# Feed-forward products by seven block products instead of eight: one inference step of a hybrid encoder on one core

## The reference

```python
for layer in range(2):
    h = rms_norm(x, norm_mix[layer])
    mix = ab_mixer(h, ...) if layer == 0 else chunk_mlp_mixer(h, ...)
    x = x + mix
    h = rms_norm(x, norm_ffn[layer])
    f, sc = conv_ffn(h, s_conv[layer], w_in_ffn[layer], ffn_conv_w[layer], ffn_conv_b[layer], w_out_ffn[layer])
    x = x + f
y = rms_norm(x, norm_final)

def conv_ffn(h, conv_hist, w_in, conv_w, conv_b, w_out):      # D_MODEL 1024, D_FF 2816
    proj = h @ w_in                                          # 1024 x 5632
    a, gate = proj[..., :D_FF], proj[..., D_FF:]
    full = concatenate([conv_hist, a])                       # along time
    conv = conv_b + sum(full[:, j:j + T] * conv_w[j] for j in range(3))
    y = (gelu(conv) * gate) @ w_out                          # 2816 x 1024
    return y, full[:, -2:]
```

## Time and profile before

| | |
|---|---|
| timed runs of the kernel before | 2838.18 us median (2835.65, 2838.18, 2838.43) |
| the profiled execution: span | 2835.0 us, 44317 instructions |
| its own time outside the span | not recorded apart; the median lies 3.2 us above the span |
| TensorE busy | 2809.9 us |
| VectorE, ScalarE, GpSimd busy | 1477.7, 707.6, 733.5 us |
| moved | 130.70 MB, 46 GB/s on average |

### The profile page before, as it was taken

The page is one execution under the profiler, slowest core; times in us unless marked ns, Lnnn a source line. Parts: engine busy times, 40 slices in busy tenths (PEclk is TensorE's granted clock), DMA queues, the critical chain, the costliest instruction groups (busy, mean ns, idle before and its releaser), DMA issues.

```text
span 2835.0 us, 44317 instructions
## 1 busy us (share of the span) xinstructions
PE 2809.9 (99%) x16164; PEld 2735.6 (96%) x16164; DVE 1477.7 (52%) x2678; ACT 707.6 (25%) x1191; POOL 733.5 (26%) x540
## 2 busy tenths in 40 slices
PE   9999999999999999999999999999999999999999
PEld 9999999999999999999888999999999999999997
DVE  3658975554444444457323755556544444444454
ACT  4424463211111111114222221214211111111114
POOL 3233325322222222223001230013422222222220
PEclk9999999999999999999999999999999999999999
DMA  4111001111111111111211111111111111111112
GB/s 146 41 43 40 24 27 48 41 42 41 44 41 41 42 43 41 41 45 45 60 51 58 34 42 41 44 41 34 52 42 41 44 41 41 44 41 41 44 48 85
DMA packets 195026, 130.70 MB, mean 46 GB/s; under 512 B 8876, under 2 KB 186741, under 8 KB 194677
## 3 DMA queue, kind: packets, MB, share of 16 engines
q1 hardware_dynamic: 194900, 129.43, 15.2%
q10 hardware_dynamic: 32, 0.01, 0.0%
HBM read 120.60 MB, written 8.81 MB: 46 GB/s over the span
## 4 chain that ended last, share of the span: by engine, by line
PE 94%; DVE 4%; issue 1%; ACT 1%; DMA 0%; POOL 0%; DVEq 0%; SPq 0%; ACTq 0%; POOLq 0%
PE bank L723 49%; PE bank L748 21%; PE bank L1246 7%; PE bank L772 3%; PE bank L884 3%; PE bank L1170 2%; PE bank L1353 2%; PE bank L919 1%; PE bank L822 1%; PE bank L1306 1%; DVE qsc L1548 1%; DVE work L2050 0%; PE bank L1138 0%; DVE sct L1569 0%; PE bank L905 0%
## 5 line engine op out<-in xcount | busy, mean ns | idle before, releaser
L2836 POOL TENSOR_TENSOR raw<-raw,vec 128x512 f32<-128x512 f32 x248 | 279.5, 1138 | 1297.2 <-DMA raw<-in_w_in_ffn 844.3
L723 PE MATMUL bank<-xh,wh 128*128 128x384 f32 x2664 | 607.2, 335 | 0.7 <-issue 0.7
L723 PE MATMUL bank<-xl,wh 128*128 128x384 f32 x2664 | 604.5, 334 | 0.0
L723 PE MATMUL bank<-xh,wl 128*128 128x384 f32 x2664 | 604.4, 334 | 0.0
L2181 ACT ACTIVATE wh<-raw 128x512 fp32r<-128x512 f32 x374 | 235.3, 629 | 1396.3 <-PE bank L723 781.1
L1398 DVE TENSOR_TENSOR wl<-raw,wh 128x512 fp32r<-128x512 f32 x374 | 283.7, 759 | 424.9 <-ACT wh L2181 424.9
L723 PEld LDWEIGHTS bank<-xh,wh 128*128 128x128 f32 x2664 | 473.6, 188 | 2.8 <-issue 1.5
L723 PEld LDWEIGHTS bank<-xl,wh 128*128 128x128 f32 x2664 | 474.6, 188 | 0.0
L723 PEld LDWEIGHTS bank<-xh,wl 128*128 128x128 f32 x2664 | 474.4, 188 | 0.0
L1424 DVE TENSOR_TENSOR xs<-bank,xs 128x384 f32<-128x384 f32 (+1 forms) x648 | 320.9, 550 | 280.3 <-PE bank L748 246.8
L748 PE MATMUL bank<-yh,wh 128*128 128x384 f32 x1152 | 265.0, 338 | 0.0
(11 more groups left out here) (340 smaller groups left out, 3369.6 us busy)
## 6 DMA issues: line engine op xcount, KB each, us to landing
raw<-in_w_in_ffn SPq DMA_DIRECT2D x176, 256.0 KB, 2.9
raw<-in_w_out_ffn SPq DMA_DIRECT2D x88, 256.0 KB, 2.7
raw<-in_w_uv_c SPq DMA_DIRECT2D x64, 256.0 KB, 2.8
raw<-in_w_in_ab SPq DMA_DIRECT2D x40, 256.0 KB, 2.9
raw<-in_w_out_c SPq DMA_DIRECT2D x32, 256.0 KB, 2.7
xtok<-in_x_prompt SPq DMA_DIRECT2D x8, 512.0 KB, 7.7
raw<-in_w_out_ab SPq DMA_DIRECT2D x16, 256.0 KB, 2.7
out_y_prompt<-otok SPq DMA_DIRECT2D x8, 512.0 KB, 2.6
```

The source lines that it names most:

```text
L723: mm = pe.matmul(ps[(sg + tb) % BANKS][:, 0:TB], w[:, place, k * P:(k + 1) * P], r[:, kk, tbs(tb)], start=kk == 0 and c == 0, stop=kk == K ...
L2836: pool.tensor_tensor(r, r, g, ALU.mult).then_inc(w_scaled, 1)
```

## The change

Both feed-forward stages are rewritten. The tokens are cut into two halves of 576 (`HT`, `T1S` and `T2S`), each matmul has 288 columns (`CH`), and PSUM is used as four pairs of banks (`psp`), 288 columns on either side of the middle of a pair.

**Up part.** 22 blocks of 256 columns (an a block, a gate block, in turn), each a product of 2 x 2 blocks: k in two halves, columns in two halves, tokens in two halves. Seven products (`UP_ORDER`) replace eight. Their x operands are x or sums of x blocks, made once per layer by VectorE (`normed`, `combos`), with x normalized and scaled by the gain first, in place, and split (`combo_high`, `combo_low`) into `cw` and `cx`, which take the room of the hidden work and of `xh`, `xl`. Four sums of the weights per block are VectorE's (`first_sums`, `up_sum`); ScalarE and VectorE combine the products as they take them out of PSUM (`up_evict`). GpSimd no longer scales weights.

**Through memory.** `xs` is stored to a scratch tensor in HBM before it is overwritten, and comes back later; all of y is stored as it is made and read back, block by block, into `yb11`, `yb22`, `yb12`, `yb21`.

**Down part.** It now follows the whole up part: seven products (`DOWN_ORDER`) of 11 steps each. A step has a weight piece or the sum of two (`w_sum`, VectorE) and a y block or the sum of two (`y_sum`, GpSimd), and 24 matmuls into four PSUM pairs; after 11 steps VectorE adds the pairs to one or two quarters of `xs` each (`down_evict`). Rings of three and four pieces hold the split operands.

**Edges.** The first product needs the norm. Stage v's split of x starts after the down part; the last layer's down part is like the first's, and the final norm follows it, with x turned by 72 transposes. The feed-forward loops are written out, with no hardware loop.

```diff
@@ TensorE
-                    for u in range(4):
-                        unit(xh, xl, n1 + 12 * i + 2 * u, g1 + 36 * i + 3 * u, n1 + 2 * u, g1 + 3 * u)
-                    down(n1 + 12 * i + 8, g1 + 36 * i + 12, n1 + 8, g1 + 12, 2 * i + (done0 + 2))
-                loop(pe, STEPS - 2, step)
...
+                def product(n, j):
+                    q, pos = UP_ORDER[j], 7 * n + j
...
+                    pe.wait_ge(f_high, done + pos + 1)
+                    pe.wait_ge(f_low, done + pos + 1)
...
+                    for k in range(4):
...
+                        for e, (w, part) in enumerate(((fh, 0), (fh, 1), (fl, 0))):
+                            for c in range(2):
+                                mm = pe.matmul(bank[:, M0 + c * CH:M0 + (c + 1) * CH], w[:, pos % RING, k * P:(k + 1) * P],
+                                               x[:, m, part, c * CH:(c + 1) * CH], start=first and k == 0 and e == 0,
...
+                for j in range(7):
+                    r0 = STEPS * j
+                    for first, last in ((0, 2), *((k, k + 1) for k in range(2, STEPS - 2)), (STEPS - 2, STEPS)):
+                        for f in range(4):
+                            for kk in range(first, last):
+                                down_step(r0 + kk, f)
@@ VectorE
+                inv_rms(1 + 2 * l)
+                dve.wait_ge(x_moved, 160 * l + 16 * KD)
+                for d in range(4):
+                    normed(d, T1S)
+                for k in range(4):
+                    combo_low(0, k)
+                for k in range(4):
+                    normed(k, T2S)
+                    normed(4 + k, T2S)
+                    normed(4 + k, T1S)
+                    combos(k)
+                    combo_low(1, k)
...
+                for pos in range(1, UPS):
+                    if 2 <= pos < 7:
+                        for k in range(4):
+                            combo_low(pos, k)
+                    if pos + 2 < UPS:
+                        up_sum(pos + 2)
...
+                    up_evict(pos - 1)
+                    convs(pos)
+                    if pos + 2 < UPS:
+                        up_low(pos + 2)
...
+                for r in range(2, DOWNS):
+                    j, kk = divmod(r + 1, STEPS)
+                    if kk == 2 and j:
+                        w_low(r)
+                        y_low(r)
+                        down_evict(j - 1)
+                        w_sum(r + 1)
+                    else:
+                        if r + 1 < DOWNS:
+                            w_sum(r + 1)
+                        w_low(r)
+                        y_low(r)
@@ GpSimd
+                for i in range(STEPS):
+                    y_prod(i)
+                for r in range(STEPS, DOWNS):
+                    y_sum(r)
+                    j, kk = divmod(r, STEPS)
...
+                    if l == 0 and j == 6 and 4 <= kk <= 9:
+                        for m in (2 * kk - 8, 2 * kk - 7):
+                            add_square(24 * 2 + m, m % 2, m % NTB, sq_b)
@@ SyncE
+                for d in range(KD):
+                    sp.wait_ge(acc_free, g0 + NTB * (d + 1))
+                    sp.dma_start(xscr[l][d], xs[:, d, :]).then_inc(x_moved, 16)
...
+                        if d >= 8:
+                            sp.wait_ge(f_low, done + UPS + step_of(d - 8) + 1)
...
+                y_tiles(yb22[:, 9:11, :], 20, 22, T2S, y_back[2])
+                for d in range(0, KD, 4):
+                    sp.dma_start(xs[:, d:d + 4, :], xscr[l][d:d + 4].rearrange("d p t -> p d t")).then_inc(x_moved, 16)
@@ the end
+            def finish(t):
...
+                for d in range(KD):
+                    mm = pe.transpose(psp[t % 4][:, d * P:(d + 1) * P], xs[:, d, t * P:(t + 1) * P], ident[:, :])
...
+                dve.scalar_tensor_tensor(otok[:, t % 2, :], psp[t % 4][:, :], fin_sums[:, t, 2:3], fin_gain[:, :],
+                                         ALU.mult, ALU.mult).then_inc(y_out, 1)
```

More of the change, by code:

```diff
@@ new lines, in ring, with y_block, up_sums, sums_of @@
+        def ring(r):
+            e = (3, 1, 2, 0)[r % 4]
+            return (fh3[:, :], fl3[:, :], flf3[:, :]) if e == 3 else (fh[:, e, :], fl[:, e, :], flf[:, e, :])
+        def y_block(b, kk):
+            if b == 21 and kk == STEPS - 1:
+                return yb21_last[:, :]
+            return {11: yb11, 12: yb12, 21: yb21, 22: yb22}[b][:, kk, :]
+        def up_sums(l, n, which):
+            return (4 * PAIRS + len(SUMMED_W) * STEPS) * l + 4 * n + which + 1
+        def sums_of(r, which):
+            j, kk = divmod(r, STEPS)
+            return STEPS * sum(q in which for q in DOWN_ORDER[:j]) + kk + 1
@@ L1393, in _ @@
+            for t in range(NT):
+                finish(t)
         @block.vector
@@ L1815, in abo @@
                         low(n0 + 4 * i + 2 * u + 1, n0 + 2 * u + 1)
-                    if not first or u:
+                    if (not first or u) and not (last and u):
                         low(n0 + 4 * i + 2 * u + 2, n0 + 2 * u + 2)
@@ new lines, in ring_free, with w_sum @@
+                def ring_free(r):
+                    if r:
+                        dve.wait_ge(f_done, done + UPS + r - 3)
+                def w_sum(r):
+                    q = DOWN_ORDER[r // STEPS]
+                    if q not in SUMMED_W:
+                        return
+                    (ra, va), (rb, vb) = (down_raw(l, down_load(r, b)) for b in range(2))
+                    dve.wait_ge(raw_loaded[ra], va)
+                    dve.wait_ge(raw_loaded[rb], vb)
+                    ring_free(r)
+                    dve.tensor_tensor(ring(r)[2], fraw[:, ra, :], fraw[:, rb, :],
+                                      ALU.subtract if q in (6, 7) else ALU.add).then_inc(f_summed, 1)
@@ L2554, in _, with abo @@
             n0, g0, t0 = PLAN.at["abo"]
-            def abo(i):
-                first = isinstance(i, int)
+            def abo(i, first=False, last=False):
                 for u in range(2):
-                    if not first or u:
+                    if (not first or u) and not (last and u):
                         for p, tk in ((2, 1), (3, 4)):
@@ L2669, in _ @@
             rms(2)
-            tail_rows(0)
             def mixing_matrix(m):
```

1272 lines of the change are left out of this document (724 added, 548 removed).

## The result

Changed kernel: **2822.02 us** median (2818.73 to 2823.6, 4 runs); before, on the same chip, 2837.48 us (2835.65 to 2838.43, 4 runs). Ratio 0.9945, 95% interval 0.9931 to 0.9959. The forecast was 2821. The profiled execution has a span of 2818.8 us, against 2835.0.

What follows compares the result with a forecast made beforehand. TensorE, busy 99% of the span, was taken as the bound. Layer 0 at 817.5 against 830.7, stage v giving back 10, and layer 1 at 831 against 845.4 made a span of 2817; 3.2 more gave 2821 us, range 2783 to 2860.

Steps and rivals of the forecast that it cites:

- 5544 matmuls a layer: Both feed-forwards: 288-column matmuls at 0.1342 us each take 744.0 us a layer, against 827.8 before.
- opening: Start of each feed-forward: products wait for the norm and VectorE's split of x; 40 us a layer.
- joint of up and down: Passage from up to down part: steps 0 and 1 end at 18.6 us instead of 9.6; 9 us a layer.
- transfers in the first stage: First down stage: 13.7 MB at 361 GB/s take 38 us against 35.4; 5 us a layer charged.
- both-sum stages: Down stages of products 1, 6 and 7: steps need 3.12 us, under 3.22; 2 us each, 6 us a layer.
- x copied away: Layer 0's opening: the copy of x to memory ends 2.5 us after the reciprocals; 2.5 us.
- squares in layer 0's last stage: Layer 0's last down stage: twelve additions of squares hold VectorE; 8 us.
- stage v: Start of stage v: x split only after the down part, norm at 32 us instead of 21.6; 10 us.
- end: After the last down step: final norm paced by two output buffers; 24 us, against 5.2 before.
- the rival on transfers: First down stage: queue moves 270 GB/s instead of 361, stage takes 51 us; total 2841, no change; chance 0.14.
- Port: Down stages: rival has VectorE and GpSimd alternate whole durations, both-sum step 3.54 us; total 2857, slower; chance 0.17.
- the rival of fewer stalls: Feed-forwards: pitch 0.1332 us, and 14 us a layer for jitter, boundaries and transfers hidden; total 2783; chance 0.18.

Runs made afterwards that it cites:

- e6: Changed kernel with layer 1's up matmuls from block 4 on cut to 256, 192 or 128 columns in turn; 0.112 us a matmul at 192 and 128.
- e3: Changed kernel with VectorE making weight piece 3's low part after the next four low parts of x in each opening; 2820.74 us, ratio 0.9937.
- e1: Changed kernel with x loaded back from memory in two halves, beside up block 3 and early in the second down stage; 2810.56 us, ratio 0.9901.
- e9: e1 with SyncE's transfers around the first down stage reordered, all of y11 ahead of the weights of steps 2 and 3; 2797.19 us, ratio 0.9860.
- e5: Changed kernel with GpSimd adding the y blocks a second time in layer 1's fifth down stage; that stage 45.9 us against 36.44, span 2833.4.
- e7: Changed kernel without GpSimd's twelve additions of squares in layer 0's last down stage; that stage 36.52 us against 45.05.
- e8: Changed kernel with six buffers instead of two for the last twelve squares at stage v's start; 2821.91 us, ratio 0.9945.
- e11: e10 plus e3's opening order, four output tiles instead of two, and a new start of stage v with six square buffers; 2772.98 us, ratio 0.9776.
- e10: e9 with the joint's work reordered on VectorE, ScalarE and TensorE, and the last block's tails copied before its taps; 2789.59 us, ratio 0.9830.

## Why the prediction came out

The total was within 1 us, the terms were not: some 33 us charged too much (22 of them the matmul's pitch in two layers) cancelled against some 35 charged too little (mainly transfers, openings and stage v). That the number came out so close is luck; that most of the 168 us would be spent again at the edges is not. By the steps of the prediction, measured in the profiled execution (layers 0, 1):

| term | predicted | measured |
|---|---|---|
| 5544 matmuls a layer | 744.0 | 732.9 (0.1322 each) |
| opening | 40 | 45.1, 46.4 |
| jitter in the up part | 3 | 0 (every block 22.21) |
| joint of up and down | 9 | 8.9, 9.2 (steps 0 and 1 end 15.2 and 15.5 after the last up product, 6.3 of it work) |
| transfers in the first stage | 5 | 12.6, 13.0 |
| both-sum stages | 6 | 1.45 + 1.51 + 1.60 = 4.6 (the third in layer 1) |
| x copied away | 2.5 | 0 |
| squares in layer 0's last stage | 8 | 8.5 |
| stage v | 10 | 16.8 |
| end | 24 | 24.2 |

- **The matmul's pitch.** I took a surplus for the weight load from the down part of before; there is none at 288 columns. The line through 384 and 512 columns (0.1733 - 0.0401 = 0.1332) was nearer, and 0.1322 lies just under the 0.133 to 0.136 that I had named as the sign. -11 us a layer, and e6 shows the floor that I feared only at 192.
- **Opening.** The parts were right (5.73 us per k against 5.8), the order of two engines was not: VectorE waited 2.4 and 0.3 us for ScalarE (e3), and its reciprocals ended 14.7 us after TensorE's last residual matmul where I had 13.5: it was 2.4 us from GpSimd's last addition (513.7) to the first of them (516.07) where I had 1.2, with the products of ones at a granted clock of 0.50. I had set the clock's cost at nothing there. The seven products were done after 67.3 and 68.6 us, against my bounds of 58 and 68.
- **Joint.** Steps 0 and 1 end 18.4 us after product 153's start (1039.44 to 1057.85) against 18.6, partly by the clock: 22 matmuls recurred every 0.24 instead of 0.13 us, 2.4 us that I hadn't in the sum; so the engines' part was smaller than charged, and the close agreement is luck too.
- **Transfers.** Here the step itself failed, not only its size: I charged 5 of the 15 us that the rival gave for 270 GB/s, since I counted bytes over the whole stage. Where TensorE waited, the queue did move 400 GB/s; it was the order that cost, x's 4.7 MB ahead of step 9's weights, and a wait of SyncE for a landing ahead of other issues. e1 and e9 take 12 and 25 us back with the same bytes. The sign that I had named for the rival on transfers, a longer first stage with waits on fraw, was there: the rival was right in size, with another cause than it named.
- **Port.** Right: both-sum stages lose only 1.5 us, so their steps fit into TensorE's 3.17; e5 and e7 confirm the price of a meeting (0.82 us at 384 columns, 1.2 at 576), and with two more additions a step it decided, as the rival says, 4.73 us in layer 0's last stage.
- **Stage v.** Low by 6.8. The group behind the norm starts 33.2 us after the stage's first product (1325.24 to 1358.47) where I had 32, and 21.6 before: 11.7 of the 16.8. What I had left out stands around it: 3.5 us ahead of the first product, in which TensorE waits until x's first tile is added up and split, and 1.6 behind the norm, where the next matmuls recur every 0.43 instead of 0.23 us, at half clock. The norm's own products took only 0.6 us more than before. How far ScalarE's order behind GpSimd's additions sets the 33.2 isn't separated: e8 freed it in part and gained nothing, e11 changed the whole start at once (-6.4 us to the reciprocal).

One sum of the prediction is off by one: the rival of fewer stalls adds up to 2782 us, not 2783.

## What to carry to other kernels

Seven products for eight gave 95 us a layer on TensorE (827.8 to 732.9), and 174 of the 190 us were spent again, most of them at edges: before the first product, at the joint, behind the reload, between the layers, and after the last step. An algorithm that takes work from the bounding engine should be costed edge by edge, and each edge as an order of queues, not as a sum of work: with nearly the same instructions and bytes, other orders and a few more buffers gained another 49 us. In these traces a weight piece asked for behind x landed behind x, so what isn't needed soon must not be asked for ahead of what is.

## Not expected of the hardware

A stream of matmuls of 192 and of 128 columns, each with its own weight load, recurs every 0.112 us, so narrowing below some 240 columns (0.112 on the line through 256 and 288) gains nothing. The Trainium skill (TensorE: Matmul & The Clock Gate, Back-to-back issue gap) gives 81 ns for 128 columns; for this type the measured 112 ns decides. With 128 columns the granted clock was 1.00 in all of the first pair of blocks. In the second and third pair it fell to 0.50 soon after a wait of 0.8 us behind the block's first product (the row at 2245.71 in experiment 6), and stayed there for 65 us although TensorE went on without a pause; it rose again only when 256-column matmuls had followed. The first pair had no such wait; waits of 0.6 us at the same place in the 256- and 192-column blocks did not bring the clock down. The cause stays open.

The first down stage of the changed kernel varied from profile to profile, 50.6 to 52.9 us in layer 0 and 52.2 to 56.2 in layer 1 in the seven profiles with the old order of transfers and of the joint, while the stages behind it that no edit touched agree to 0.1 us. So a single profile's first stage is known to some 4 us only, and the gains of e1 in it (8 and 7 us) are the more certain for exceeding that. Whether the full queue makes the timed runs uneven isn't shown: those of the changed kernel spread by 4.9 us, of e9 by 1.4, but of e10, with e9's transfers, by 6.7.
